# Attention to the memory as three fp32r products, with the probabilities scaled on ScalarE

## What is computed

```python
def memory_cross_attention(h, mem_n, w_mem_q, w_mem_kv, w_mem_o):
    q = jnp.einsum("bsd,de->bse", h, w_mem_q).reshape(B, S, MEM_HEADS, MEM_HEAD_DIM)
    kv = jnp.einsum("bmd,de->bme", mem_n, w_mem_kv)
    k = kv[..., :D_MODEL].reshape(B, M, MEM_HEADS, MEM_HEAD_DIM)
    v = kv[..., D_MODEL:].reshape(B, M, MEM_HEADS, MEM_HEAD_DIM)
    s = jnp.einsum("bshd,bmhd->bhsm", q, k).astype(jnp.float32) * (MEM_HEAD_DIM ** -0.5)
    p = jax.nn.softmax(s, axis=-1).astype(v.dtype)
    o = jnp.einsum("bhsm,bmhd->bshd", p, v).reshape(B, S, D_MODEL)
    return jnp.einsum("bse,ed->bsd", o, w_mem_o)
```

## Time and profile before

| what | us |
|---|---|
| median of 3 runs | 1483.13 (1480.7 to 1483.78) |
| profiled execution | 1481.8 |
| its span, first to last instruction | 1480.0 |
| TensorE busy in the span | 1440.3 (97%) |
| VectorE, ScalarE, GpSimd busy | 833.5, 552.0, 988.7 |
| TensorE's share of the chain that ended last | 87% |
| mean granted TensorE clock, of full speed | 0.998 |

### The profile page before, as it was taken

One profiled execution on the slowest core, in us unless ns is written; L12 is line 12 of the kernel. 1 busy time (PEld: TensorE's weight loads), 2 busy tenths in 40 slices (PEclk: granted clock), 3 DMA queues, 4 the chain that ended last, 5 costly groups with the idle time before them and its releaser, 6 DMA issues.

```text
span 1480.0 us, 18618 instructions
## 1 busy us (share of the span) xinstructions
PE 1440.3 (97%) x6987; PEld 1169.2 (79%) x6987; DVE 833.5 (56%) x1302; ACT 552.0 (37%) x1075; POOL 988.7 (67%) x398
## 2 busy tenths in 40 slices
PE   3999999999999999999999999999999999999997
PEld 3888777778888888888898844789789888888886
DVE  6998144443665655566744786441516555465655
ACT  3201134332554434444333386452424523333214
POOL 1867454445678889888567995365154989788653
PEclk9999999999999999999999999999999999999999
DMA  9875221222543332322443200133024323232131
GB/s 346 301 269 211 100 85 58 86 105 95 173 143 111 114 114 93 107 98 73 156 136 100 85 1 1 63 130 122 1 86 143 114 87 113 86 114 86 58 98 73
DMA packets 103385, 167.88 MB, mean 113 GB/s; under 512 B 3917, under 2 KB 61185, under 8 KB 102785
## 3 DMA queue, kind: packets, MB, share of 16 engines
q1 hardware_dynamic: 100176, 160.45, 31.5%
q10 hardware_dynamic: 3121, 6.26, 1.3%
HBM read 161.97 MB, written 4.72 MB: 113 GB/s over the span
## 4 chain that ended last, share of the span: by engine, by line
PE 87%; DVE 8%; ACT 3%; DMA 1%; issue 1%; DVEq 0%; SPq 0%; ACTq 0%
PE bank L910 26%; PE bank L911 26%; PE bank L912 26%; DVE bank L2054 2%; DMA ada_w<-in_w_ada 1%; DVE smx L2514 1%; DVE x L2050 1%; PE bank L1371 1%; PE bank L1428 1%; PE bank L1447 1%; PE bank L1171 1%; DVE bank L2050 1%; ACT junk L1540 1%; PE bank L1194 1%; DVE facc L2050 1%
## 5 line engine op out<-in xcount | busy, mean ns | idle before, releaser
L910 PE MATMUL bank<-ht_hi,w_hi 128*128 128x512 f32 (+1 forms) x1200 | 442.7, 369 | 0.5 <-DVE ht_lo L2050 0.3
L912 PE MATMUL bank<-ht_lo,w_hi 128*128 128x512 f32 (+1 forms) x1200 | 440.0, 367 | 0.0
L911 PE MATMUL bank<-ht_hi,w_lo 128*128 128x512 f32 (+1 forms) x1200 | 440.0, 367 | 0.0
L758 POOL TENSOR_TENSOR w_lo<-w_raw,w_hi 128x2048 fp32r<-128x2048 f32 x83 | 388.7, 4683 | 6.9
L756 POOL TENSOR_SCALAR w_hi<-w_raw 128x2048 fp32r<-128x2048 f32 x83 | 162.3, 1955 | 340.8 <-DMA w_raw<-in_w_in 108.8
L910 PEld LDWEIGHTS bank<-ht_hi,w_hi 128*128 128x128 f32 x1200 | 226.4, 189 | 41.5 <-DVE ht_lo L2050 1.8
L912 PEld LDWEIGHTS bank<-ht_lo,w_hi 128*128 128x128 f32 x1200 | 226.4, 189 | 37.2
L911 PEld LDWEIGHTS bank<-ht_hi,w_lo 128*128 128x128 f32 x1200 | 226.5, 189 | 36.7 <-issue 0.5
L808 POOL TENSOR_TENSOR dn_lo<-dn_raw,dn_hi_all 128x1024 fp32r<-128x1024 f32 x77 | 184.8, 2422 | 49.3 <-ACT dn_hi_all L1738 49.2
L2054 DVE SCALAR_TENSOR_TENSOR uc<-bank,par,uc 128x511 f32<-128x511 f32 x88 | 66.0, 750 | 128.4 <-ACT uc L1992 125.2
L822 POOL TENSOR_TENSOR dn_raw<-dn_raw 128x1024 f32<-128x1024 f32 x44 | 105.9, 2408 | 18.1 <-DMA dn_raw<-in_w_mlp_out 7.3
(11 more groups left out here) (302 smaller groups left out, 2402.7 us busy)
## 6 DMA issues: line engine op xcount, KB each, us to landing
w_raw<-in_w_in SPq DMA_DIRECT2D x27, 1024.0 KB, 5.0
ada_w<-in_w_ada SPq DMA_DIRECT2D x48, 512.0 KB, 7.1
w_raw<-in_w_up SPq DMA_DIRECT2D x22, 1024.0 KB, 4.9
w_raw<-in_w_mlp_in SPq DMA_DIRECT2D x16, 1024.0 KB, 5.6
dn_raw<-in_w_mlp_out SPq DMA_DIRECT2D x28, 512.0 KB, 4.6
w_raw<-in_w_out SPq DMA_DIRECT2D x8, 1024.0 KB, 5.0
w_raw<-in_w_mem_kv SPq DMA_DIRECT2D x8, 1024.0 KB, 5.3
dn_raw<-in_w_down SPq DMA_DIRECT2D x16, 512.0 KB, 5.2
```

The costliest lines, as they stand in the source:

```text
L758: g.tensor_tensor(w_lo[:, r], w_raw[:, r], w_hi[:, r].bitcast(F32), ALU.subtract).then_inc(slab_split, 1)
L910: inc_free(pe.matmul(o, ah, bh, start=start, stop=False))
L911: pe.matmul(o, al, bh, start=False, stop=False)
L912: return pe.matmul(o, ah, bl, start=False, stop=stop)
```

## The change

The products of the attention to the memory are put into the three-product form. A new `three` issues the three products without `inc_free`; `mm3` calls it. ScalarE casts the high halves of `mem_k` and `mem_v`, which take the places of `mt_lo` and `mt_hi`; GpSimd subtracts the low halves in place, behind the split of the third `mem_q` slab. ScalarE's copy of `qm` becomes a cast, and VectorE makes `qm_lo` and frees the tiles. ScalarE scales the probabilities, behind the four exponentials of the head, when VectorE has the reciprocal (`pm_inv`). The turned probabilities are cast by ScalarE, and VectorE makes `ptm_lo` in the step `t` and frees the tiles. New buffers are `qm_lo` and two `ptm_lo`.

```diff
@@ -430,12 +433,16 @@
 
         ph = ExitStack()
-        qm = sb("qm", [P, DC, T], where=ph)
+        qm_hi = sb("qm_hi", [P, DC, T], F32R, where=ph)
         pm = sb("pm", [P, 2, NT, NM], where=ph)
-        ptm = sb("ptm", [P, MT, T], where=ph)
+        ptm = sb("ptm", [P, MT, T], F32R, where=ph)
         gain5 = sb("gain5", [P, D], where=ph)
-        ptm_odd = sb("ptm_odd", [P, MT, T], where=ph)
+        ptm_odd = sb("ptm_odd", [P, MT, T], F32R, where=ph)
         ptm_of = (ptm, ptm_odd)
+        qm_lo = sb("qm_lo", [P, DC, T], F32R, where=ph)
+        ptm_lo = [sb(f"ptm_lo{i}", [P, MT, T], F32R, where=ph) for i in range(2)]
+        mem_k_hi = mt_lo
+        mem_v_hi = mt_hi[:].rearrange("p (a b) n -> p a (b n)", a=MT)
         ph.close()
...
@@ -859,7 +867,12 @@
                 g.wait_ge(sm_inv, i + 1)
                 g.tensor_scalar(out, out, smx[:, 2, j, qt:qt + 1], 1.0, ALU.mult, ALU.mult).then_inc(sm_p_pool, 1)
-            split_all(n, S0["ffn"] + 2)
+            split_all(n, S0["mem_q"] + 3)
+            g.wait_ge(kv_hi, 1)
+            g.tensor_tensor(mem_k_lo[:], mem_k[:], mem_k_hi[:].bitcast(F32), ALU.subtract).then_inc(kv_lo, 1)
+            g.wait_ge(kv_hi, 2)
+            g.tensor_tensor(mem_v_lo[:], mem_v[:], mem_v_hi.bitcast(F32), ALU.subtract).then_inc(kv_lo, 1)
+            split_all(S0["mem_q"] + 3, S0["ffn"] + 2)
             g.wait_ge(xn5_ready, NT)
...
@@ -906,10 +919,15 @@
                 return n % RING
 
+            def three(o, ah, al, bh, bl, start, stop):
+                first = pe.matmul(o, ah, bh, start=start, stop=False)
+                pe.matmul(o, al, bh, start=False, stop=False)
+                return first, pe.matmul(o, ah, bl, start=False, stop=stop)
+
             def mm3(o, ah, al, bh, bl, start, stop):
-                inc_free(pe.matmul(o, ah, bh, start=start, stop=False))
-                pe.matmul(o, al, bh, start=False, stop=False)
-                return pe.matmul(o, ah, bl, start=False, stop=stop)
+                first, last = three(o, ah, al, bh, bl, start, stop)
+                inc_free(first)
+                return last
 
...
@@ -1425,8 +1443,9 @@
                     t.wait_free(pe)
                     for c in range(2):
-                        ins = pe.matmul(t.ap[:, 0:NM], qm[:, 2 * h + c, qt * P:qt * P + P], mem_k[:, 2 * h + c, :],
-                                        start=c == 0, stop=c == 1)
+                        q = slice(qt * P, qt * P + P)
+                        _, ins = three(t.ap[:, 0:NM], qm_hi[:, 2 * h + c, q], qm_lo[:, 2 * h + c, q],
+                                        mem_k_hi[:, 2 * h + c, :], mem_k_lo[:, 2 * h + c, :], c == 0, c == 1)
                     ins.then_inc(t.full, 1)
...
@@ -1444,12 +1463,13 @@
                     t.wait_free(pe)
                     for kc in range(MT):
-                        ins = pe.matmul(t.ap[:], mem_v[:, kc, h * MHD + c * P:h * MHD + c * P + P], ptm_of[h % 2][:, kc],
-                                        start=kc == 0, stop=kc == MT - 1)
+                        d = slice(h * MHD + c * P, h * MHD + c * P + P)
+                        _, ins = three(t.ap[:], mem_v_hi[:, kc, d], mem_v_lo[:, kc, d], ptm_of[h % 2][:, kc],
+                                  ptm_lo[h % 2][:, kc], kc == 0, kc == MT - 1)
                     ins.then_inc(t.full, 1)
 
             all_taken(range(T0["mem_q"], T0["mem_q"] + DC))
-            pe.wait_ge(k_back, 16)
+            pe.wait_ge(kv_lo, 2)
             for what, h in ATTM_ORDER:
...
@@ -1876,13 +1896,17 @@
                                                    bias=smx[:, 0, h % 2, qt:qt + 1],
                                                    accum_out=smx[:, 1, h % 2, qt:qt + 1]), tile=t)
+                        for qt in range(NT):
+                            act.wait_ge(pm_inv, NT * h + qt + 1)
+                            st.done(act.activation(p_of(h)[:, qt], p_of(h)[:, qt], ACT.Copy,
+                                                   scale=smx[:, 2, h % 2, qt:qt + 1]), sm_p)
                     elif what == "t":
                         for kc in range(keys // P):
                             t = Tile(tt["t", h] + kc)
                             t.wait_full(act)
                             if h >= 2 and kc == 0:
                                 Tile(tt["o", h - 2] + len(out_of(h)) - 1).wait_full(act)
-                            st.done(act.copy(pt[h % 2][:, kc], t.ap[:]), tile=t)
+                            st.done(act.copy(pt[h % 2][:, kc], t.ap[:]), ptm_made)
                     elif what == "m":
...
@@ -1964,8 +1988,14 @@
             act.dma_start(gain5[:], A["norm_ffn_pre_2"].partition_broadcast(P)).then_inc(gain5_loaded, 16)
             load_table(ACT.Exp)
+            act.wait_ge(k_back, 16)
+            st.after()
+            st.done(act.copy(mem_k_hi[:], mem_k[:]), kv_hi)
+            st.done(act.copy(mem_v_hi, mem_v[:]), kv_hi)
             for m in range(DC):
-                copy_out(T0["mem_q"] + m, qm[:, m])
+                t = Tile(T0["mem_q"] + m)
+                t.wait_full(act)
+                st.done(act.copy(qm_hi[:, m], t.ap[:]), qm_made)
             softmax_attention(ATTM_ORDER, TTM, MH, NM, lambda h: pm[:, h % 2], ptm_of, lambda h, qt: SCM, NT * H1,
...
@@ -2497,8 +2527,12 @@
                             fill()
                             Tile(tiles["z", h] + qt).wait_taken(v)
-                            recip(smx[:, 2, h % 2, qt:qt + 1], smx[:, 1, h % 2, qt:qt + 1])
-                            ts(p_of(h)[:, qt], p_of(h)[:, qt], smx[:, 2, h % 2, qt:qt + 1], None, ALU.mult, sem=sm_p)
+                            recip(smx[:, 2, h % 2, qt:qt + 1], smx[:, 1, h % 2, qt:qt + 1], pm_inv)
+                    elif what == "t":
+                        for kc in range(MT):
+                            t = Tile(tiles["t", h] + kc)
+                            v.wait_ge(ptm_made, MT * h + kc + 1)
+                            tt(ptm_lo[h % 2][:, kc], t.ap[:], ptm_of[h % 2][:, kc].bitcast(F32), ALU.subtract, tile=t)
                     elif what == "o":
...
@@ -2555,6 +2589,10 @@
                 tt(ht_lo[:, c], ay[:, c], ht_hi[:, c].bitcast(F32), ALU.subtract, part_lo)
             post_and_norm(lambda m: post_psum(2, m, T0["w_out2"]), "nt4", col(V_NMEM, 8), ht_hi, ht_lo)
+            for m in range(DC):
+                v.wait_ge(qm_made, m + 1)
+                t = Tile(T0["mem_q"] + m)
+                tt(qm_lo[:, m], t.ap[:], qm_hi[:, m].bitcast(F32), ALU.subtract, tile=t)
             softmax_attention(ATTM_ORDER, TTM, MH, NM, lambda h: pm[:, h % 2], lambda h, qt: (-SCM, None), NT * H1, 2 * PAIRS,
```

More of the change, by code:

```diff
@@ L403, in build @@
             p1_sum = sb("p1_sum", [P, 2, T], where=lend)
-        mem_k = sb("mem_k", [P, DC, NM])
-        mem_v = sb("mem_v", [P, MT, D])
+        with ExitStack() as lend:
+            mem_k = sb("mem_k", [P, DC, NM], where=lend)
+            mem_v = sb("mem_v", [P, MT, D], where=lend)
+        mem_k_lo = sb("mem_k_lo", [P, DC, NM], F32R)
+        mem_v_lo = sb("mem_v_lo", [P, MT, D], F32R)
         mt_hi = sb("mt_hi", [P, DC, NM], F32R)
@@ L473, in build @@
         squared, mlp_slab_hi, mlp_hi, mlp_sums = (sem(n) for n in ("squared", "mlp_slab_hi", "mlp_hi", "mlp_sums"))
+        qm_made, ptm_made, kv_hi, kv_lo, pm_inv = (sem(n) for n in ("qm_made", "ptm_made", "kv_hi", "kv_lo", "pm_inv"))
         memory_kept, mt_back, k_back = sem("memory_kept"), sem("mt_back"), sem("k_back")
```

## The result

The changed kernel takes 1485.76 us, the median of 22 runs (1483.14 to 1489.66). In the same runs the kernel before takes 1482.91 (1479.04 to 1484.81). The ratio is 1.0030, with a 95% interval of 1.0022 to 1.0038: slower, by more than the 0.2% that a measurement here can tell. The medians alone would give 1.0019, because the times of the kernel before fall into two groups and its median lies in the upper one; the means, 1486.15 and 1481.94, are 4.2 us apart. The profiled execution took 1488.56 us, its span is 1486.6.

What follows compares the result with a forecast made beforehand. TensorE was taken to bound the kernel; its 5.4 us saving would be lost to the VectorE, ScalarE, VectorE series and late entrance, ending 3.4 us later: 1481.8 to 1485.2, or 1486.5 on the median's scale; range 1482.5 to 1490.0.

Steps and rivals of the forecast that it cites:

- The likeliest case: Attention to the memory: engines in series set the stage with the clock at 1.00; 1486.5 us, 70%.
- the series VectorE, ScalarE, VectorE: Each head's maxima, then exponentials, scalings and cast, then subtractions run one after another; 7.08 and 8.69 us a head.
- TensorE alone: TensorE's work in the memory attention: four heads take 25.9 us where the stage took 31.28, 5.4 us off.
- Entrance: Between last mem_q projection and first scores: one more VectorE subtraction frees the last tile, scores 0.72 us late.
- Halves of mem_k and mem_v: ScalarE's casts and GpSimd's subtractions ahead of the stage cost nothing, with 1.3 us of cover left.
- GpSimd comes late: Rival: GpSimd's two passes at twice their time delay the fourth mem_q slab; 6.4 us late, 1489.5 us, chance 4%.
- Scalings, casts, subtractions: ScalarE and VectorE per head: four scalings 1.60 us (0.40 each), a cast 0.59, two subtractions 1.60.
- the walk: Step-by-step timing of the stage from scores at 1043.99 to head 3's values ending at 1077.98, against 1074.55.
- The sum: Whole kernel: the stage ends 3.4 us later, giving 1485.2 us, or 1486.5 on the scale of the median.
- TensorE stays the bound: Rival: the series does not bind, the stage ends 4.7 us early at 1069.9; 1478.5 us, faster, chance 10%.
- the case of a fall in the holes: Rival: TensorE's holes around head 3's turn halve the clock, 1.7 us more; 5.1 us late, 1488.2 us, chance 16%.
- The scalings by the Trainium skill's rule: With three products but the scalings left on VectorE, the stage would end 1.9 us later and not 3.4.

Runs made afterwards that it cites:

- e5: Changed kernel, same instructions, ScalarE casting a turned head before scaling the next and VectorE moving head 0's and 1's value subtractions later: 1479.92 us, ratio 0.9991.
- e7: Changed kernel with the orders of e5, and TensorE waiting before each head's scores for that head's two mem_q tiles only: 1477.95 us, ratio 0.9975.
- e1: Changed kernel with the 16 scalings moved back to VectorE, behind each reciprocal, three products kept: 1485.79 us, ratio 1.0023.
- e4: Changed kernel with ScalarE casting the turned head before scaling the following head, VectorE's order left as changed: 1484.20 us, ratio 1.0011.
- e6: Changed kernel with every 128x256 scaling on ScalarE issued as two of 128x128: 1489.51 us, ratio 1.0048.
- e10: Changed kernel with the one-column products near 171 us split into two bursts, far ahead of the change: 1484.77 us, ratio 1.0021.
- e3: Changed kernel with 12 otherwise unused products filling TensorE's hole ahead of the turn of head 3: 1484.93 us, ratio 1.0022.
- e11: Kernel e7 with the one-column products near 171 us split into two bursts: 1477.69 us, ratio 0.9978.

## Why the prediction was right, and where its steps stand

*The likeliest case and its mechanism held.* Forecast were 1486.5 us and a stage set by the series VectorE, ScalarE, VectorE; measured were 1485.76 and that chain. The series from one head's first subtraction to the next was put at 7.08 and 8.69 us; the rows say 7.05 (1055.19 to 1062.24) and 8.64 (to 1070.88). That the order and not the work is the price is shown by e5: the same instructions in another order take 7.1 us less in the stage, 5.0 of them at full clock (33.81 against 28.85).

*TensorE alone.* Three score products per 0.36 and three value products per 0.68 at full clock, as forecast. Of the 5.4 us saved there, e5 keeps 2.4 in the stage (2.3 with like ends); 2.1 go into the waits that its two rows show, and the rest was not traced. The later entrance, 0.7 us, comes on top of that until e7.

*Entrance.* Forecast 0.72, measured 0.73, by the row forecast: one more subtraction of 0.70.

*Halves of mem_k and mem_v.* Free, as forecast. GpSimd's second pass ended at 1019.4, and its wait for the slab of 1.63 us shows the cover that was left (forecast 1.3). Rival "GpSimd comes late": no.

*Scalings, casts, subtractions.* Four scalings took 1.70, 0.40 from start to start, the value taken between the bounds of 0.29 and 0.61. VectorE's idle time ahead of the subtractions was 1.63, forecast some 1.6; the hole ahead of the turn 2.79, forecast about 3. One small reading of the walk is off: the 0.31 us between the end of work and the first maximum are 0.28 by its rows (1043.27 + 0.86, then 1044.41).

*The sum.* Entrance and order at full clock make 0.73 + 33.81 - 31.28 = 3.3 us (3.4 with like ends), forecast 3.4. Rival "TensorE stays the bound": no, TensorE waits for VectorE or ScalarE at five places in the stage.

*The clock.* This is the step that did not hold. The likeliest case had the granted clock at 1.00, and the case of a fall in the holes had 16%, because "the hole is shorter than that stretch and work surrounds it". The clock fell in the profile of the changed kernel, and in those of e1, e4, e6 and e10, all that keep a hole of 2.8 to 3.5 us there; it did not fall where the hole was filled (e3) or gone (e5, e7, e11). "TensorE: Matmul & The Clock Gate" of the Trainium skill, What's actually happening, has the clock halved after idleness; the rows of these holes agree. Ahead of the fall near 176 the profile has TensorE busy without a pause. The price of a fall was put at 1.7 us; the profiles show 2.1 in the changed kernel, 1.7 in e4, 1.2 in e6, 1.0 in e1 and 0.2 in e10. So the mechanism of the likeliest case and that of this rival were both at work. That the median rose by 2.9, so near the forecast of 3.4, is partly luck: 12 of the 22 runs of the kernel before are at 1482.86 or above and the next is at 1481.18, so its median just fell into the upper group. By the means the difference is 4.2, and without the fall near 176 it is 4.7, both between the 3.4 of the series alone and the 5.1 of the series with the clock.

*The scalings by the Trainium skill's rule.* "ScalarE: Activation LUTs" of the Trainium skill, Rules for kernel authors, would keep the multiplications on VectorE; the profile of e1, which does so, agrees. The scalings on VectorE were forecast at 1.5 us less, and e1 gives 1.3 less in the series at full clock, but the ratio doesn't show it (1.0023 against 1.0030, intervals that overlap). And in e5 and e7 the scalings stay on ScalarE in kernels that are not slower than before: the place of the scalings mattered less than that of the casts, whose place alone (e4) takes 3.0 us off the stage at full clock. The orders of e5 with the scalings on VectorE were not tried.

## What to carry to other kernels

Before splitting an operand into halves in a pipelined attention, write out one step of each engine's queue and follow the loop through all engines: two engines that are busy 22.7 of 37 us can still set the pace if each waits once per head for the other. Where a new instruction makes one engine wait for another, put the instruction that it waits for ahead of the long work in that other queue; here this, and a wait per head in place of one wait for all, turned a loss of 0.3% into a gain of 0.25%. And count a hole on TensorE of some 3 us as dearer than its length, since the clock can be at half for the work behind it.

## What the runs showed of the hardware that was not expected

The clock fell behind a hole of 2.77 to 3.51 us, or at its end, in all five profiles that had one, and behind none of the pauses of 1.7 us at the entrance, in seven profiles (1.00 over 1040 to 1052). What a fall costs is not fixed: 0.2 us in e10 and 2.1 in the changed kernel, by how long the half clock lasts (a mean of 0.89 and of 0.79 over 16 us) and by how much of it lies on work that nothing else delays.

The same falls explain most of the spread of the kernel before. Thirty-two instructions of one-column products in a row (3.6 us) brought the granted clock to 0.57 over 176 to 180 in its profile and to 0.50 in that of the changed kernel, while in that of e7 the same 32 left it at 1.00. Divided into two bursts with two products of 512 columns between them, they left it at 1.00 in the three profiles taken, and the range of the times went from 5.3 us (23 runs) to 1.6 (11 runs).
